# Modulation section 5 taken out of the state space stage, and sections 6 to 10 summed by VectorE in the feed-forward steps

## The reference, cut to what matters

```python
c_act = jax.nn.silu(c)
for i in range(DEPTH):                      # DEPTH = 2
    mod = c_act @ w_ada[i] + b_ada[i]       # [1, 1024] @ [1024, 6144]: 24 MB of weights for each layer
    sh1, sc1, g1 = mod[:, :D], mod[:, D:2*D], mod[:, 2*D:3*D]
    sh2, sc2, g2 = mod[:, 3*D:4*D], mod[:, 4*D:5*D], mod[:, 5*D:]
    h = modulate(rms_norm(x, norm_g[i, 0]), sh1, sc1)
    h = s5_mixer(h, ...) if i % 2 == 0 else mla_mixer(h, ...)
    x = x + g1[:, None, :] * rms_norm(h, norm_g[i, 1])
    h = modulate(rms_norm(x, norm_g[i, 2]), sh2, sc2)
    h = dense_swiglu(h, ...) if i % 2 == 0 else moe_swiglu(h, ...)
    x = x + g2[:, None, :] * rms_norm(h, norm_g[i, 3])
```

## Time and profile before

| What | Value |
|---|---|
| median of 3 runs | 1058.44 us (1055.41 to 1060.71) |
| the profiled execution | 1057.97 us, of it the profile's span 1055.9 us |
| state space stage (to the GLU's first product) | 0 to 138.74 us |
| GLU, residual, norm | 138.74 to 197 us |
| feed-forward steps | 197 to 402 us |
| residual, norm, MLA, router | 402 to 541 us |
| experts and the end | 541 to 1055.9 us |

### The profile page before, as it was taken

One profiled execution on the slowest core, in us unless ns is written; L12 is line 12 of the kernel. 1 busy time (PEld: TensorE's weight loads), 2 busy tenths in 40 slices (PEclk: granted clock), 3 DMA queues, 4 the chain that ended last, 5 costly groups with the idle time before them and its releaser, 6 DMA issues.

```text
span 1055.9 us, 17162 instructions
## 1 busy us (share of the span) xinstructions
PE 975.8 (92%) x6618; PEld 806.5 (76%) x6619; DVE 808.2 (77%) x1078; ACT 634.4 (60%) x787; POOL 55.3 (5%) x116
## 2 busy tenths in 40 slices
PE   0786699899999999989989999999999999999995
PEld 0464388798898997867878888888888888888884
DVE  7989884445345556787568898989989898898995
ACT  4437174534234445565657867878687786867763
POOL 3003300000000000000200000000000000000000
PEclk9988799999999999999989999999999999999998
DMA  9898975757786866540559999999999999899961
GB/s 258 311 346 239 224 248 208 260 179 261 263 305 236 296 256 260 214 161 1 181 164 379 317 379 366 340 385 322 391 340 362 373 329 402 311 389 358 335 266 61
DMA packets 134243, 297.67 MB, mean 282 GB/s; under 512 B 9493, under 2 KB 40842, under 8 KB 133914
## 3 DMA queue, kind: packets, MB, share of 16 engines
q1 hardware_dynamic: 126026, 282.92, 74.9%
q0 software_dynamic: 4080, 8.48, 2.8%
q10 hardware_dynamic: 4064, 5.26, 1.7%
HBM read 291.06 MB, written 3.16 MB: 279 GB/s over the span
## 4 chain that ended last, share of the span: by engine, by line
PE 83%; DVE 11%; ACT 3%; issue 2%; DMA 1%; SPq 0%; DVEq 0%; ACTq 0%
PE ps L638 24%; PE ps L640 23%; PE ps L639 23%; PE ps L682 2%; PE ps L1166 1%; PE ps L1025 1%; PE ps L1139 1%; PE ps L1140 1%; PE ps L815 1%; DVE s_out_map L1927 1%; PE ps L1117 1%; PE ps L727 1%; PE ps L794 1%; PE ps L804 1%; DMA mod_rows<-ada_wide 0%
## 5 line engine op out<-in xcount | busy, mean ns | idle before, releaser
L2292 DVE TENSOR_TENSOR w_lo<-raw,w_hi 128x2048 fp32r<-128x2048 f32 x162 | 365.6, 2287 | 36.3 <-ACT w_hi L1621 36.3
L1621 ACT ACTIVATE w_hi<-raw 128x2048 fp32r<-128x2048 f32 x162 | 302.9, 1912 | 0.0
L1720 DVE TENSOR_TENSOR w_lo<-raw,w_hi 128x2048 fp32r<-128x2048 f32 (+3 forms) x59 | 131.6, 2249 | 92.0 <-ACT w_hi L1291 91.0
L638 PE MATMUL ps<-w_hi,xe_hi 128*128 128x512 f32 x448 | 177.4, 396 | 0.9 <-DVE xe_lo L2252 0.9
L640 PE MATMUL ps<-w_hi,xe_lo 128*128 128x512 f32 x448 | 175.3, 391 | 0.0
L639 PE MATMUL ps<-w_lo,xe_hi 128*128 128x512 f32 x448 | 174.7, 390 | 0.0
L1291 ACT ACTIVATE w_hi<-raw 128x2048 fp32r<-128x2048 f32 (+3 forms) x59 | 109.1, 1875 | 71.7 <-DMA raw<-in_ffn_w_in 69.1
L638 PE MATMUL ps<-act_hi,w_hi 128*128 128x256 f32 x352 | 101.1, 287 | 1.9 <-DVE act_lo L1888 1.9
L639 PE MATMUL ps<-act_lo,w_hi 128*128 128x256 f32 x352 | 99.5, 283 | 0.0
L640 PE MATMUL ps<-act_hi,w_lo 128*128 128x256 f32 x352 | 99.5, 283 | 0.0
L638 PEld LDWEIGHTS ps<-w_hi,xe_hi 128*128 128x128 f32 x448 | 84.2, 188 | 17.9 <-issue 1.1
(11 more groups left out here) (425 smaller groups left out, 1540.9 us busy)
## 6 DMA issues: line engine op xcount, KB each, us to landing
raw<-in_moe_w_in SPq DMA_DIRECT2D x112, 1024.0 KB, 7.0
raw<-in_moe_w_out SPq DMA_DIRECT2D x56, 1024.0 KB, 8.4
raw<-in_w_ada SPq DMA_DIRECT2D x48, 1024.0 KB, 9.5
raw<-in_ffn_w_in SPq DMA_DIRECT2D x44, 512.0 KB, 7.9
raw<-in_ffn_w_out SPq DMA_DIRECT2D x11, 1024.0 KB, 10.9
raw<-in_ssm_w_glu SPq DMA_DIRECT2D x16, 512.0 KB, 11.6
raw<-in_mla_w_o SPq DMA_DIRECT2D x4, 1024.0 KB, 8.6
raw<-in_mla_w_uq SPq DMA_DIRECT2D x3, 768.0 KB, 7.0
```

What stands on the lines that cost most here:

```text
L638: mm(dst, st[0], mv[0], start=first, stop=False)
L1621: af(HI[:, (V_MOE + m) % RING, :], RAW[:, (RAW_OF_W[V_MOE] + m) % RING, :], cp).then_inc(hi_done, 1)
L1720: tt_(LO[:, slot, 0:w], RAW[:, RAW_OF_W[v] % RING, 0:w], HI[:, slot, 0:w].bitcast(F32), ALU.subtract)\
L2292: tt_(LO[:, slot, :], RAW[:, (RAW_OF_W[V_MOE] + m) % RING, :], HI[:, slot, :].bitcast(F32), ALU.subtract)\
```

## The change

- The ada pieces that stand ahead of the GLU's weights are 0 to 19 instead of 0 to 23. Ada 20 to 23 (section 5) come in feed-forward step 0, where 24 to 27 stood: TensorE sums them after the GLU. Every step 1 to 10 has two ada pieces (24 to 43); 44 to 47 stay after the last.
- SP issues its part of both chunk map transfers ahead of w unit 4 (r = 24).
- TensorE no longer has ada 20 to 23 around `strips(1)`. Between `outputs(0)` and `outputs(1)` it runs `keep_warm(8, 7)`.
- In steps 1 to 10 DVE sums ada 24 to 43, two at the start of each step (`ada_weighted`): for either half of a piece it multiplies 128 x 1024 numbers by a column of `c` and adds them to `ACC`. The first half of a section is a `tensor_scalar`, the other seven are `scalar_tensor_tensor`. At the end of every second step TensorE adds `ACC` over the partitions with four matmuls against ones (`ada_total`).
- `wide`, `mod_rows` and `mod_columns` of sections 5 to 10 move: `wide` by one section per step, `mod_columns(10)` to the MLA stage, ahead of `keep_warm(14, ...)`; `mod_rows(10)` ahead of `mod_rows(11)`.
- `gate_store(5)` comes after the first load of `GROW` on the POOL queue. The mask's semaphore is counted with the other constants.

```diff
+SUMMED = (6, 7, 8, 9, 10)
+EARLY_ADA = 20
 def ADA_PER_STEP(t):
-    return 4 if t == 0 else 2 if t <= FSTEPS - 3 else 0
+    return 4 if t == 0 else 2
 def raw_stream():
-    s = [("ada", n) for n in range(24)]
+    s = [("ada", n) for n in range(EARLY_ADA)]
...
 # SP
-                if r in (26, 27):
-                    m_blocks(sp, r - 26, M_ROWS["sp"], m_in[r - 26])
+                if r == RAW_OF_W[4]:
+                    for part in range(2):
+                        m_blocks(sp, part, M_ROWS["sp"], m_in[part])
...
 # POOL
-            gate_store(5)
 
             pool.wait_ge(yt_ok, DT)
             pool.wait_ge(gate_out[0], 16)
             pool.dma_start(GROW[:, :], scr_gate[0, :].partition_broadcast(P)).then_inc(gate_in, 16)
 
+            gate_store(5)
             section_rows(6)
...
 # TensorE
+            def ada_total(s):
+                pe.wait_ge(ada_used, 4 * (s + 1))
+                pe.wait_ge(wide_ok, s - 1)
+                if s - 2 not in GATES:
+                    pe.wait_ge(mod_ok, sum(1 for i in range(s - 1) if i not in GATES))
+                for c4 in range(4):
+                    last = mm(PS[32 * c4:32 * c4 + 32, ada_bank(s), 0:256], ONE32[:, :], ACC[:, c4 * 256:(c4 + 1) * 256],
+                              start=True, stop=True)
+                last.then_inc(ada_sum, 1)
...
             strips(0)
             mod_columns(3)
-            ada(20)
-            ada(21)
             strips(1)
-            ada(22)
-            ada(23)
             outputs(0)
+            pe.wait_ge(strip_ok, 4)
+            keep_warm(8, 7)
             outputs(1)
...
             keep_warm(10, 7)
-            for n in range(24, 28):
+            for n in range(20, 24):
                 ada(n)
...
-                    if ft == 0 and t and t % 2 == 0 and 5 + t // 2 not in GATES:
-                        mod_columns(5 + t // 2)
+                    if ft == 0 and t and t % 2 == 0 and 4 + t // 2 not in GATES:
+                        mod_columns(4 + t // 2)
                 if t:
                     ffn_down(t - 1)
-                for n in range(26 + 2 * t, 26 + 2 * t + (ADA_PER_STEP(t) if t else 0)):
-                    ada(n)
+                if t % 2 == 0 and 5 + t // 2 in SUMMED:
+                    ada_total(5 + t // 2)
...
-            keep_warm(14, 4)
+            mod_columns(10)
+            keep_warm(14, 5)
...
 # ACT
-            wide(5)
...
-                if t % 2 == 0 and t < FSTEPS - 1:
-                    wide(6 + t // 2)
+                if t % 2 == 0:
+                    wide(5 + t // 2)
...
 # DVE
-            mod_rows(5)
...
+            def ada_weighted(n):
+                s, kk = divmod(n, 4)
+                wait_raw(dve, RAW_OF_ADA[n])
+                dve.wait_ge(ada_used, n)
+                if n == 4 * SUMMED[0]:
+                    dve.wait_ge(n_lo, DT)
+                    v_.memset(ONE32[:, :], 1.0)
+                elif kk == 0:
+                    dve.wait_ge(ada_sum, SUMMED.index(s))
+                for k in range(2):
+                    w, c = RAW[:, RAW_OF_ADA[n] % RING, k * D:(k + 1) * D], CB[:, 2 * kk + k, 0:1]
+                    if kk == 0 and k == 0:
+                        link_(v_.tensor_scalar(ACC[:, :], w, c, None, ALU.mult))
+                        continue
+                    ins = v_.scalar_tensor_tensor(out=ACC[:, :], in0=w, scalar=c, in1=ACC[:, :], op0=ALU.mult, op1=ALU.add)
+                    if k == 0:
+                        link_(ins)
+                ins.then_inc(ada_used, 1)
...
                 if t == FSTEPS - 2:
                     rope_angles()
+                for n in range(22 + 2 * t, 22 + 2 * t + (ADA_PER_STEP(t) if t else 0)):
+                    ada_weighted(n)
...
                     if ft == 1 and t % 2:
-                        mod_rows(6 + t // 2)
+                        mod_rows(5 + t // 2)
...
+            mod_rows(NSEC - 2)
             mod_rows(NSEC - 1)
```

More of the change, by code:

```diff
@@ L66, in ADA_PER_STEP @@
 def ADA_PER_STEP(t):
-    return 4 if t == 0 else 2 if t <= FSTEPS - 3 else 0
+    return 4 if t == 0 else 2
 def raw_stream():
-    s = [("ada", n) for n in range(24)]
+    s = [("ada", n) for n in range(EARLY_ADA)]
     w = iter(range(10 ** 6))
     s += [("w", next(w)) for _ in range(8)]
-    ada = list(range(24, 48))
+    ada = list(range(EARLY_ADA, 48))
     for step in range(FSTEPS + 1):
@@ L202, in program @@
         RES_END = at("res_tmp_end", [P, TT, D], 48 + 8 * ((V_ALL - 5) % RING))
+        ACC = at("ada_acc", [P, D], 152)
         WIDE = at("ada_wide", [P, 2, 256], 196)
@@ L262, in program @@
         IOTA = at("iota", [P, P], kc + 2.625)
+        ONE32 = at("ones_32", [P, 32], 156)
         IOTI = nc.alloc_sbuf_tensor_at("iota_i", [P, P], I32, offset=BASE + int(142 * KB))
@@ L299, in program @@
             "at_ok const_ok rows_in a_in bn_in cn_in x_ld pos_ld")
-        CONST = dict(ident=1, shift=2, iota=3, tri=4)
+        CONST = dict(ident=1, shift=2, iota=3, mask=4, tri=5)
         rows_ps, vec_ok, ldt_ok, ct_ps, ct_ok, cact_ok, cb_ok = sems(
@@ L604, in _ @@
             pool.affine_select(out=MASK[:, P:], in_=MASK[:, P:], compare_op=ALU.is_ge, fill=NEG, base=0,
-                               pattern=[[-1, P]], channel_multiplier=1).then_inc(mask_ok, 1)
+                               pattern=[[-1, P]], channel_multiplier=1).then_inc(const_ok, 1)
             pool.wait_ge(o_mm, H)
@@ L665, in ada_bank @@
             def ada_bank(s):
-                return 4 + s % 2 if s < 6 else 6 + s % 2
+                return 4 + s % 2 if s < 5 else 6 + s % 2
             def ada(n):
@@ L673, in ada @@
                     pe.wait_ge(cb_ok, 1)
-                if kk == 0 and s >= 2 and s not in (6, 7):
+                if kk == 0 and s >= 2 and s != 5:
                     old = s - 2
@@ L685, in ada @@
                 last.then_inc(ada_used, 1)
+            def ada_total(s):
[7 more added lines that the diff above has]
+                last.then_inc(ada_sum, 1)
             def mod_columns(s):
                 pe.wait_ge(mrow_ok, s + 1)
+                bank = 4 if s == 10 else ada_bank(s)
                 for half in range(2):
-                    last = mm(PS[:, ada_bank(s), 256 + half:256 + half + 7:2], MROW[0:4, s % 2, half * P:(half + 1) * P],
+                    last = mm(PS[:, bank, 256 + half:256 + half + 7:2], MROW[0:4, s % 2, half * P:(half + 1) * P],
                               IDENT[0:4, 0:4], start=True, stop=True)
@@ L971, in _ @@
                         pe.wait_ge(p_f32, 5)
+                        pe.wait_ge(mod_ok, 8)
                     for b in range(3):
@@ L1337, in wide @@
             def wide(s):
-                act.wait_ge(ada_used, 4 * (s + 1))
+                act.wait_ge(*((ada_sum, SUMMED.index(s) + 1) if s in SUMMED else (ada_used, 4 * (s + 1))))
                 if s >= 2:
                     act.wait_ge(row_in[s % 2], 16 * (s // 2))
-                af(WIDE[:, s % 2, :], PS[:, (4 if s < 6 else 6) + s % 2, 0:256], cp).then_inc(wide_ok, 1)
+                af(WIDE[:, s % 2, :], PS[:, (4 if s < 5 else 6) + s % 2, 0:256], cp).then_inc(wide_ok, 1)
                 act.wait_ge(wide_ok, s + 1)
@@ L1850, in mod_columns @@
             def mod_columns(s):
-                bank = (4 if s < 6 else 6) + s % 2
+                bank = 4 if s == 10 else (4 if s < 5 else 6) + s % 2
                 n = sum(1 for i in range(s + 1) if i not in GATES)
@@ L2090, in _ @@
                     if ft == 1 and t % 2:
-                        mod_rows(6 + t // 2)
-                    if ft == 1 and t and t % 2 == 0 and 5 + t // 2 not in GATES:
-                        mod_columns(5 + t // 2)
+                        mod_rows(5 + t // 2)
+                    if ft == 1 and t and t % 2 == 0 and 4 + t // 2 not in GATES:
+                        mod_columns(4 + t // 2)
                 split_to(va + 6 if t else V_FFN + 5)
@@ L2159, in _ @@
                 v_.tensor_copy(VV[:, 1, 4 * b:4 * b + 4, :], kv[:, :, NOPE:]).then_inc(kv1_ok, 1)
-            dve.wait_ge(mask_ok, 1)
+            dve.wait_ge(const_ok, CONST["mask"])
             dve.wait_ge(q_rope, 2)
```

2 lines of the change are left out of this document (1 added, 1 removed).

## The result

| | before | after |
|---|---|---|
| median of 4 runs each | 1056.93 us (1055.22 to 1060.71) | 1039.65 us (1038.82 to 1040.87) |
| the profiled execution, of it the span | 1057.97 us, 1055.9 us | 1038.83 us, 1036.9 us |

The ratio is 0.9843, with a 95% interval of 0.9824 to 0.9861. The forecast was 1040.

A forecast was written before the change was run, and what follows sets the result against it. The prediction took TensorE to bound the feed-forward steps and make the state space stage late. From the profiled 1057.97 us, -5.6 - 12.6 + 0.3 gave 1040.1, stated as 1040 us; range 1036.5 to 1048.

The forecast's parts named there:

- part 1: State space stage: GLU starts 6.9 us earlier without ada 20 to 23, less 1.3 us for the clock; -5.6 us.
- part 2: Feed-forward steps: TensorE loses 14.9 us of ada pieces and gains 2.3 us of `ada_total`; -12.6 us.
- the end of the steps: Step 10: MLA's first unit split at 17.5 us, wanted at 17.9; cost 0.3 us, bounds 0 and about 3.
- That VectorE becomes what is late: End of the state space stage: VectorE, no longer TensorE, sets the GLU's start, 6.9 us earlier.
- The clock's price: GLU's first products may run at 1.2 GHz after TensorE idles; 1.3 us taken, bounds 0 and 5.2.
- Rival 1: State space stage gives little or nothing, as instruction block ends fall elsewhere but still cost; 1045.7 us, chance 0.2.
- The chunk map's second part: State space stage: its transfer should land by about 118 us, where before the last landed near 122.
- VectorE's step 9: Feed-forward step 9, with the rope angles: VectorE needs 12.56 + 5.3 = 17.9 us, 0.7 over the 17.2.
- Units 3t+2 and 3t+3: Feed-forward steps: VectorE splits these w units by 7 and 9.8 us, wanted at 17.2; room of 7 us.
- rival 3: Feed-forward steps: VectorE becomes late and part 2 gives about half; 1046 or up to 1052 us, chance 0.08.
- rival 4: Feed-forward steps: VectorE's half pieces cost far more than 1.29 us; at 3.2 us each, 1080.6 us; chance 0.03.

The follow-up runs named there:

- best: Changed kernel with `keep_warm(16, 7)` added ahead of `strips(0)` and `keep_warm(10, 5)` for `keep_warm(14, 5)` in the MLA stage; 1038.82 us, ratio 0.9832.
- strip_after_turn: Changed kernel with ScalarE copying the first strips out after its last turned part, not before; 1040.66 us, ratio 0.9849.
- map_late: Changed kernel with w unit 4 loaded between SP's two parts of the chunk map; 1039.19 us, ratio 0.9856.
- no_warm: Changed kernel without the wait and `keep_warm(8, 7)` between `outputs(0)` and `outputs(1)`; 1039.02 us, ratio 0.9839.
- dve_x2: Changed kernel with one more zero-factor `scalar_tensor_tensor` on VectorE for each of the 35; 1068.82 us, ratio 1.0121 against the kernel before.
- pe_sums: Changed kernel with TensorE summing ada 24 to 43 in steps 1 to 10, in place of VectorE's sums and `ada_total`; 1069.58 us, ratio 1.0125.
- pe_6_9: Changed kernel with TensorE summing sections 6 to 9 in steps 1 to 8, VectorE only section 10; 1058.68 us, ratio 1.002.
- old_state: Changed kernel with the state space stage as in the kernel before, the feed-forward part kept; 1046.28 us, ratio 0.9894.
- before_shift: Kernel before with `keep_warm(16, 7)`, 32 more matmul records, ahead of `strips(0)`; 1056.71 us, ratio 1.0007.
- pe_sums_late: Changed kernel with TensorE summing ada 24 to 43, and MLA's first unit split behind step 10's second low part; 1066.43 us, ratio 1.0088.

## Why the prediction was right, step by step

**The sum.** 1040 was forecast, 1039.65 measured. The terms, read from the two profiles: part 1 -5.6 for -6.0; part 2 -12.6 for -13.3 + 0.5 = -12.8; the end of the steps +0.3 for 0; 0.2 us in the later stages have no name. Each term is right within 0.5 us, and not only their sum. That the sum came within 0.35 us is partly luck: it says 17.9 us less, the profiled executions differ by 19.1 and the medians by 17.3, and the median of before alone was 1058.44 over three runs and 1056.93 over four.

**The state space stage.** That VectorE becomes what is late held. The GLU came 6.55 us earlier, not 6.9: the second half of the scan was done at 122.49, and not at 121.98, since `strips(0)` ran at 1.2 GHz (3.67 us for 128 records; 2.03 at the full clock in `best`), ScalarE's turned part came late and VectorE waited 1.73 us for it. In `best` that wait is 0.71 us and the scan is done at 121.81. I had taken the time up to the scan's end as unchanged. The clock's price was 0.5 us and not 1.3: the windows of after have the clock at 0.72 and 0.85 around the GLU's start, and it was back by 133.3. By the Trainium skill's page "TensorE: Matmul & The Clock Gate" (section "What's actually happening"), which has the throttled state as the default, the part was worth 1.7 us in the prediction; the trace shows the effect (0.72 where the engine has just idled 2.97 us) at a twelfth of what the part gave.

```profile
128.00:132.00 4.00, 3.73 (x22) 3.56 (x22) 4.00 (x9) 1.42 (x3) 0.19 (x1) 0.72 0.75 242
132.00:136.00 4.00, 3.95 (x16) 3.13 (x16) 2.97 (x5) 3.97 (x4) 0.40 (x1) 0.85 0.74 188
```

The two errors, 0.35 and 0.8, are of opposite signs.

What the runs do not separate is whether the pieces' own time or the lost gaps gave the 6 us. An estimate from the earlier trace rows: without the gaps of 4.16 and 4.89 us, and with the pieces in place, before would have its outputs done near 115.8 and 125.6, both ahead of VectorE (122.0 and 127.8 in the prediction). Without the pieces behind `strips(1)` (1.06 + 2.68 us) but with both gaps the second would be done near 130.9, too late. So by this estimate, which leaves the map's transfers out, losing the gaps alone would do and losing the pieces alone would not. Why the shifted block ends cost so little stays open; on this point the forecast had luck.

**Rival 1**, the block ends. They fell where they were counted: 91 records into L815 of `outputs(0)` was forecast, `strip_after_turn` and `map_late` show an end after 92; near the end of L815 of `outputs(1)`, and it is 5 records ahead of it. Their price was wrong in the rival: in after the first shows no gap and the second 0.27 us, in the other two kernels they are 0.6 to 1.1 us each, not 4.9. The chunk map's second part landed at 120.7, not 118, and TensorE waited 0.94 us for it, within its room. That room was real: `no_warm` has 4.0 us of wait for the same part and the same end.

**Part 2.** A step is 17.1 us for 17.2, and 18.35 with `ada_total` (0.47 forecast) and `mod_columns` (0.7) in it. VectorE's step 9 was forecast at 17.9 us and took 15.01: the 12.56 of the earlier trace rows held splits of the steps beside it (five splits lie in part or whole in that window, 7.57 us, and three, 6.09 us, in after's), which is 1.5 us of the 2.9. Another 0.6 is that step 9 begins a section: its two pieces cost 4.7 us and not the 5.3 that I added. The rest is rope work that now stands ahead of the window. Units 3t+2 and 3t+3 were split 6.5 us ahead of the step's end (room 7). So rival 3 did not come (it does in `dve_x2`), and rival 4's price of a half piece was false.

**The end of the steps** came out as forecast (room 0.4 by my count, 1.3 measured). But I priced it at 0.3 with bounds to 3, as a small thing. The runs show that it is the tightest place of the change: 2.5 us more of VectorE's work in every step cost 5.1 us there in one wait, and a slot freed at the end of step 10 costs 12.0. The term of 0.3 came out at 0 with only 1.3 us to spare. Also, the prediction valued VectorE's work at TensorE's own time alone. `pe_sums` says that the same twenty pieces on TensorE cost 30 us, of which 16.3 are its time and the rest a slot freed late, with the clock behind that gap. In the kernel before this price was not paid, since steps 9 and 10 had no ada pieces.

## What to carry to other kernels

When work leaves a saturated engine, count its time one for one, but also ask when its buffer now comes free and which load waits for that buffer: here the wait for the load behind the last piece was 12.0 us, against 16.3 us for the work of all twenty pieces. An engine's room is the smallest one of the stretch, so look at the last step, where other work follows, and not at the repeated one. A gap on TensorE inside a run of matmuls, with no semaphore in it, may be the end of an instruction block: count records from one to the next (here 127 or 128, or a multiple) before blaming the work around it.

## What was not expected of the hardware

- TensorE's gaps without a semaphore lie 127 or 128 matmul records with their loads apart, or a multiple of that. The long ones were 4.16, 4.89, 2.66, 4.62, 3.74 and 3.54 us (two each in before, `old_state` and `before_shift`), all with the DMA engines at a share of 1.09 to 1.14. But there was one of 1.14 us at about the same share (1.09) in `strip_after_turn`; one of 1.74 us in before and one of 2.29 us in `pe_6_9` with the share at 0.05 and 0.04; and 0.3 to 0.8 us with it at 0.00 (`after`, `map_late`, `pe_sums_late`). A busy queue goes with all that are over 2.3 us; it is not enough for a long one, nor needed for one of 2 us. What sets the length stays open.
- The clock of a stretch with gaps is not the same from kernel to kernel. With idle gaps of 4.03, 1.59 and 1.09 us ahead of it, `no_warm` started the GLU with the clock at 1.00 (window 128 to 132), while after, with eight unused products more, had 0.72 there. `keep_warm(8, 7)` bought nothing.
- A matmul stream that resumed after a wait of 4.1 us (`pe_6_9`) ran at 0.50 for some 5 us, a cost of 2.3 us on top of the wait.
